# The down projection of 15 experts by seven block products, placed between the next expert's columns

## The chip, the cores and the metric

The kernel runs on one core of a Trainium2 chip. The metric is the device time of one execution in microseconds; lower is better.

## What is computed

One layer of a denoising backbone (a mixer of a long convolution and retention, then a mixture of experts, then a norm). The change is in the experts. Each of 16 experts takes the 256 latent tokens of 2048 and the 16 context tokens of 128 that have the highest affinity to it:

```python
vals, idx = lax.top_k(aff.T, cap)
xs = xt[idx]
hid = jax.nn.silu(jnp.einsum("ecd,edf->ecf", xs, p["w_e_gate"])) * jnp.einsum("ecd,edf->ecf", xs, p["w_e_up"])
ye = jnp.einsum("ecf,efd->ecd", hid, p["w_e_down"]) * vals[..., None].astype(h.dtype)
y = jnp.zeros((T, D), h.dtype).at[idx.reshape(-1)].add(ye.reshape(-1, D))
...
x = x + g2 * ec_moe(h, p)
...
y_sample = rmsnorm(xs, norm_f_g)
```

All three weights of an expert are 1024 x 1024 in float32, so the down projection is a product of 256 x 1024 by 1024 x 1024. Products are kept near float32 accuracy in three parts: an operand a is split in a rounded high part and a low part a - high, and high x high, high x low and low x high are summed.

## The kernel before

The phase of the experts (`phase_experts`) is the last of seven and takes about the last 1,250 us. Its 16 experts follow each other, unrolled in Python. On each engine `body` writes the queue of one expert by hand, and semaphores (`Steps` objects such as PW, VW, AW, VG, AH, VD, CP, one count for each named step) tie the queues together. Each engine works its queue in order.

**The columns.** The hidden side of an expert is made in eight tiles f of 128 hidden channels. For each, TensorE makes a gate column and an up column (`column`), 24 matmuls with 272 columns (256 latent and 16 context tokens) each, into PSUM banks pg and pu, from split weights (`w_high_gu`, `w_low_gu`, ring of four) and the split, transposed tokens (`xT_high`, `xT_low`). ScalarE applies silu to the gate (L3198, `act_g`); VectorE multiplies it with the up column (L3468 latent part into `full`, L3469 context part); ScalarE copies the product to its rounded high part (L3209, `hid_high`); VectorE subtracts for the low part (L3477, `hid_low`).

**The weights.** A row of weights is 128 x 1024. SP loads 24 of them for each expert in the order of STREAM (g0, u0, then g, u and the down row of the tile before). ScalarE copies each to its high part (`split`, L3151), VectorE subtracts for the low part (`split`, L3375), both two positions of the stream ahead of TensorE.

**The down projection.** `down(e, f)` adds hidden tile f times down row f to all four PSUM banks pd (2 token halves x 2 output halves), 12 matmuls of 512 columns. It stands one tile behind the columns of the same expert; the last two stand behind the context product (`down_context`, L3094, on unsplit weights). At the end of the expert VectorE multiplies the four banks by the affinity and the gate of the layer into `ye` (L3502), and the context rows likewise (L3490).

**Beside it.** In each expert VectorE also counts the places of the tokens of the expert after next (L3335, L3338, L3352), TensorE transposes the next expert's tokens, and ScalarE and VectorE split those (L3163, L3384, L3381). POOL issues the DMAs that gather tokens and that add `ye` to the sum `xacc` in memory (L3612); only when one expert's sums have landed may the next one's be issued.

**The last expert.** Once expert 14's rows are added, POOL loads `xacc` in 17 tiles (L3566). ScalarE squares each tile (L3171) and takes the root of the mean for batches of tiles (L3182), VectorE scales (L3409), POOL stores (L3570). The rows that expert 15 itself touches are done last (L3415, L3225, L3424, L3597). This work stands in the queues between the steps of expert 15's columns.

## Time and profile before

| | us |
|---|---|
| median of 3 runs | 3275.08 (3274.41 to 3278.94) |
| the profiled execution | 3273.48 |
| its span, first to last instruction | 3271.6 |
| TensorE busy in the span | 3085.6 (94%) |
| VectorE busy | 1911.9 (58%) |
| ScalarE busy | 1413.3 (43%) |

Busy times are unions of the records of an engine. A TensorE record is longer than the distance to the next one, since matmuls overlap, so prices are taken from the distance between starts. L and a number is a line of the kernel. The mean clock that TensorE was granted is 0.967 of its full rate.

### The profile page before, as it was taken

The page shows a single profiled execution, that of the slowest core. Times are in us where ns is not written, and L with a number is a line of the kernel's source. Part 1 is how long each engine was busy: PE and PEld are TensorE (multiplying, and loading weights), DVE is VectorE, ACT ScalarE, POOL GpSimd, SP SyncE. Part 2 cuts the span into 40 slices and gives each one's busy share as a digit, 9 for nine tenths or more (in the row PEclk, how much of TensorE's full clock was granted, in tenths as well). Part 3 has the DMA queues.
Part 4 walks back from the last instruction along what each step waited for, and adds up shares of the span by engine and source line. Part 5 has one row for each costly group of instructions (what it writes and reads, how often), then busy time and mean ns, then how long its engine had stood idle before and what let it go on. Part 6 is the DMA issues. An engine that isn't in the chain of part 4 may idle for free. (4 is left out here: it accounts for less than half of the span.)

```text
span 3271.6 us, 52938 instructions
## 1 busy us (share of the span) xinstructions
PE 3085.6 (94%) x20253; PEld 2673.1 (82%) x20253; DVE 1911.9 (58%) x3135; ACT 1413.3 (43%) x2101; POOL 526.9 (16%) x440
## 2 busy tenths in 40 slices
PE   7899999899979879999999984999999999999997
PEld 2378888798945779999997764999999999899996
DVE  5544443433345578776755558666666666666656
ACT  4633333422244145564644541444444444444446
POOL 1011111000023334101000003121111111112212
PEclk9999999999989889999999996999999999999998
DMA  8733332421199976767656443565655555565668
GB/s 329 264 113 114 126 106 90 153 60 60 57 313 361 362 241 219 232 218 229 216 171 202 155 149 131 197 204 193 199 195 192 193 185 183 183 208 195 198 205 311
DMA packets 334757, 630.73 MB, mean 193 GB/s; under 512 B 28408, under 2 KB 209912, under 8 KB 329865
## 3 DMA queue, kind: packets, MB, share of 16 engines
q1 hardware_dynamic: 308575, 568.47, 50.7%
q0 software_dynamic: 16992, 54.88, 5.6%
q10 hardware_dynamic: 8976, 4.46, 0.5%
q8 instruction: 143, 2.34, 0.3%
q14 instruction: 71, 0.58, 0.1%
HBM read 490.16 MB, written 137.56 MB: 192 GB/s over the span
## 5 line engine op out<-in xcount | busy, mean ns | idle before, releaser
L71 PE MATMUL experts_bank<-experts_xT_high,experts_w_high_gu 128*128 128x272 f32 x2048 | 596.2, 291 | 6.4 <-DVE experts_w_low_gu L3375 3.9
L73 PE MATMUL experts_bank<-experts_xT_high,experts_w_low_gu 128*128 128x272 f32 x2048 | 591.4, 289 | 0.0
L72 PE MATMUL experts_bank<-experts_xT_low,experts_w_high_gu 128*128 128x272 f32 x2048 | 589.6, 288 | 0.0
L71 PEld LDWEIGHTS experts_bank<-experts_xT_high,experts_w_high_gu 128*128 128x128 f32 x2048 | 386.1, 189 | 12.8 <-ACT experts_act_g L3198 5.3
L72 PEld LDWEIGHTS experts_bank<-experts_xT_low,experts_w_high_gu 128*128 128x128 f32 x2048 | 387.1, 189 | 4.6
L73 PEld LDWEIGHTS experts_bank<-experts_xT_high,experts_w_low_gu 128*128 128x128 f32 x2048 | 386.0, 188 | 0.0
L3375 DVE TENSOR_TENSOR experts_w_low_gu<-experts_w_raw_gu,experts_w_high_gu 128x1024 fp32r<-128x1024 f32 x256 | 302.6, 1219 | 25.3 <-ACT experts_w_high_gu L3151 20.5
L2146 PE MATMUL merge_bank<-merge_rows_high,merge_w_gates_high 128*128 128x272 f32 x896 | 261.4, 292 | 9.1 <-DVE merge_rows_low L2303 5.9
L3151 ACT ACTIVATE experts_w_high_gu<-experts_w_raw_gu 128x1024 fp32r<-128x1024 f32 x256 | 256.8, 1045 | 14.0 <-DMA experts_w_raw_gu<-in_w_stream 14.0
L2148 PE MATMUL merge_bank<-merge_rows_high,merge_w_gates_low 128*128 128x272 f32 x896 | 260.6, 291 | 0.0
L2147 PE MATMUL merge_bank<-merge_rows_low,merge_w_gates_high 128*128 128x272 f32 x896 | 259.2, 289 | 0.0
L73 PE MATMUL experts_bank<-experts_w_high_d,experts_hid_low 128*128 128x512 f32 x512 | 204.0, 398 | 0.0
L71 PE MATMUL experts_bank<-experts_w_high_d,experts_hid_high 128*128 128x512 f32 x512 | 203.8, 398 | 0.0
L3198 ACT ACTIVATE experts_act_g<-experts_bank 128x272 f32<-128x272 f32 x128 | 50.8, 397 | 352.4 <-PE experts_bank L73 352.3
L72 PE MATMUL experts_bank<-experts_w_low_d,experts_hid_high 128*128 128x512 f32 x512 | 202.5, 396 | 0.0
L3468 DVE TENSOR_TENSOR experts_full<-experts_bank,experts_act_g 128x256 f32<-128x256 f32 x128 | 54.4, 425 | 253.1 <-issue 150.6
L71 PE MATMUL hyin_pz<-hyin_hT_high,hyin_w_high 128*128 128x436 f32 (+1 forms) x480 | 176.2, 367 | 14.0 <-DVE hyin_hT_low L1421 14.0
L2146 PEld LDWEIGHTS merge_bank<-merge_rows_high,merge_w_gates_high 128*128 128x128 f32 x896 | 170.1, 190 | 9.8 <-issue 9.8
L3536 POOL TENSOR_TENSOR experts_spare<-experts_spare 128x1 f32<-128x1 f32 x46 | 29.0, 642 | 920.1 <-DVE experts_ye L3502 769.9
L72 PE MATMUL hyin_pz<-hyin_hT_low,hyin_w_high 128*128 128x436 f32 (+1 forms) x480 | 172.9, 360 | 0.0
L73 PE MATMUL hyin_pz<-hyin_hT_high,hyin_w_low 128*128 128x436 f32 (+1 forms) x480 | 172.9, 360 | 0.0
L2147 PEld LDWEIGHTS merge_bank<-merge_rows_low,merge_w_gates_high 128*128 128x128 f32 x896 | 170.4, 190 | 0.0
(435 smaller groups left out, 7256.4 us busy)
## 6 DMA issues: line engine op xcount, KB each, us to landing
experts_w_raw_gu<-in_w_stream SPq DMA_DIRECT2D x256, 512.0 KB, 4.6
experts_w_raw_d<-in_w_stream SPq DMA_DIRECT2D x128, 512.0 KB, 6.7
merge_rows_b<-scratch_hT SPq DMA_DIRECT2D x52, 544.0 KB, 5.4
filters_wm<-in_w_mod SPq DMA_DIRECT2D x12, 2048.0 KB, 11.2
merge_rows_t<-scratch_row_sums SPq DMA_DIRECT2D x36, 544.0 KB, 6.7
merge_y<-scratch_yhy SPq DMA_DIRECT2D x32, 544.0 KB, 5.1
merge_y<-scratch_yret SPq DMA_DIRECT2D x32, 544.0 KB, 4.7
x_early<-in_xT SPq DMA_DIRECT2D x17, 512.0 KB, 5.2
```

Of the source, the lines that this page charges most:

```text
L71: pe.matmul(out, lhs[0], rhs[0], start=start, stop=False)
L72: pe.matmul(out, lhs[0], rhs[1], start=False, stop=False)
L73: return pe.matmul(out, lhs[1], rhs[0], start=False, stop=stop)
L2146: pe.matmul(out, high, rh[:, w, q, :], start=not onto and q == 0, stop=False, skip_group_check=onto)
L2147: pe.matmul(out, high, rl[:, w, q, :], start=False, stop=False, skip_group_check=onto)
L2148: mm = pe.matmul(out, low, rh[:, w, q, :], start=False, stop=q == HK - 1, skip_group_check=onto)
L3151: act.activation(wh[kind][:, n % RINGS[kind], :], raw[kind][:, r, :], ACT.Copy).then_inc(*AW.inc(name))
L3198: act.activation(act_g[:], pg[:, 0:SLOTS], ACT.Silu).then_inc(*AG.inc(f"g{f}"))
L3375: v.tensor_tensor(wl[kind][:, w, :], raw[kind][:, n % STAGES[kind], :], wh[kind][:, w, :].bitcast(F32), ALU.subtract).then_inc(*VW.inc(name))
L3468: v.tensor_tensor(full[:, f % 2, :], pu[:, 0:CAP], act_g[:, 0:CAP], ALU.mult).then_inc(*VG.inc(f"m{f}"))
L3536: g.tensor_tensor(spare[:, column:column + 1], spare[:, 0:1], spare[:, 0:1], ALU.add)\
```

## The change

Experts 0 to 14 make the down projection as a 2 x 2 block product in seven products of quarter size instead of eight (a scheme of Strassen's kind in Winograd's form). The blocks are the two token halves and the two halves of the hidden channels of `hid` on one side, and the two halves of the hidden channels (rows f 0 to 3 and 4 to 7) and of the output channels of the weight on the other. Expert 15 keeps `down` by rows.

- A product is 4 tiles x 3 parts = 12 matmuls of 128 x 128 by 128 x 512. The seven weight operands are b11, b21, b22 (plain blocks) and t1 to t4 (sums of blocks).
- VectorE makes the four weight sums in place in the raw down rows, 128 x 4 x 512 each (`block_sum`), after the context product has read the rows. Each operand is then split in two halves of 128 x 1024 (14 splits in place of 8), in a ring of three.
- VectorE makes four sums of the hidden blocks for each of the tiles 4 to 7 (`hidden`, four instructions of 128 x 128); the high copy and the low part of these tiles are 128 x 768.
- The products of expert e stand in TensorE's queue behind columns 0, 1, 3, 5, 6, 7 and 8 of expert e + 1 (BEHIND). Products are added up in PSUM where they can be, else ScalarE copies them out (`copied`, three of 128 x 512), and VectorE adds and scales (`summed`, `gated`). The addition to memory of expert e so begins in slot 9 of expert e + 1.
- The context rows are multiplied by the gate by VectorE (four instructions of 16 x 256) and by the affinity by ScalarE.
- The stream of SP holds only gate and up rows; the eight down rows of an expert are loaded in its slots 6 to 9 (ROWS_AT). POOL gathers the tokens of the next expert before, not after, it adds the rows of the last one.
- The final tiles: new buffers, batches of 4, 4, 4 and 5, squares from slot 12 of expert 15, the tiles 8 to 16 behind its last column.

A slot i is one column (i even: gate, odd: up) and what stands behind it.

```diff
+LEAD, RING, RING_D = 2, 4, 3
+OPERANDS = ["b11", "b21", "t1", "t2", "t3", "t4", "b22"]
+PARTS = [f"{name}{i}" for name in OPERANDS for i in range(2)]
+BEHIND = {0: 0, 1: 1, 3: 2, 5: 3, 6: 4, 7: 5, 8: 6}
+SPLIT_AT = {1: [3], 2: [4, 5], 4: [6, 7], 5: [8], 6: [9, 10], 7: [11, 12], 8: [13]}
+SPLIT_NEXT = {13: 0, 14: 1, 15: 2}
+D_FIRST = (1, 6, 7, 8)
...
-        SQUARES = {1: (0, 2), 2: (2, 5), 3: (5, 8), 4: (8, 10), 5: (10, 13), 6: (13, 15)}
-        SCALED = {3: (0, 3), 4: (3, 5), 5: (5, 8), 6: (8, 10), 7: (13, NT)}
+        SQUARES = {12: (0, 4), 14: (4, 8)}
+        SCALED = {13: (0, 4), 15: (4, 8)}
+        ROWS_AT = {6: (0, 1), 7: (2, 3), 8: (4, 5), 9: (6, 7)}
+        PASSED_AT = {0: (0, 6), 1: (6, 9), 3: (9, 13), 5: (13, NLAT)}
+        DOWN_AT = {11: 0, 12: 1, 13: 2, 14: 3, 15: 4}
...
+                def block_product(e, j):
+
+                    to = pd[:, (0, 1, 2, 0, 0, 0, 2)[j], :]
+                    onto = j > 2
...
+                    for i in range(2):
+                        n = 2 * j + i
+                        w = ring_d(e, n)
+                        pe.wait_ge(VP.sem, VP.at(e, PARTS[n]))
+                        for q in (2 * i, 2 * i + 1):
+                            high, low = hh[:, q, j, :], hl[:, q, j, :]
+                            right = slice(512 * (q % 2), 512 * (q % 2) + 512)
+                            pe.matmul(to, high, dh[:, w, right], start=not onto and q == 0, stop=False, skip_group_check=onto)
+                            pe.matmul(to, high, dl[:, w, right], start=False, stop=False, skip_group_check=onto)
+                            mm = pe.matmul(to, low, dh[:, w, right], start=False, stop=q == HALF - 1, skip_group_check=onto)
+                        mm.then_inc(*DP.inc(PARTS[n]))
...
+                            else:
+                                act.wait_ge(VG.sem, VG.at(e, f"w{f}"))
+                                act.wait_ge(DP.sem, DP.at(e - 1, "b221"))
+                                act.activation(hh[:, f - HALF, 1:7, :], sums[:], ACT.Copy).then_inc(*AH.inc(f"h{f}"))
...
+                def block_sum(e, name):
+
+                    if name == "t1":
+                        for f in range(HALF):
+                            v.wait_ge(dld[f], 16 * (e + 1))
+                        v.wait_ge(PC.sem, PC.at(e, "context"))
+                        v.wait_ge(VP.sem, VP.at(e, "b111"))
+                        to, a, b = quarter("b11"), quarter("t3"), quarter("b11")
...
+                    v.tensor_tensor(to, a, b, ALU.subtract).then_inc(*TP.inc(name))
...
+                    v.tensor_tensor(sums[:, 3, :], full[:, q, 0, :], full[:, q, 1, :], ALU.subtract).then_inc(*VG.inc(f"x{f}"))
+                    done("m")
+                    v.tensor_tensor(sums[:, 1, :], full[:, q, 1, :], sums[:, 4, :], ALU.add).then_inc(*VG.inc(f"z{f}"))
+                    done("z")
+                    v.tensor_tensor(sums[:, 2, :], sums[:, 1, :], full[:, q, 0, :], ALU.subtract).then_inc(*VG.inc(f"y{f}"))
+                    done("y")
+                    v.tensor_tensor(sums[:, 5, :], sums[:, 0, :], sums[:, 2, :], ALU.subtract).then_inc(*VG.inc(f"w{f}"))
+
+                def low(e, f):
+
+                    steps = VE if final(e) else VG
+                    v.wait_ge(AH.sem, AH.at(e, f"h{f}"))
...
+                    for i in range(NS):
+                        f = i // 2
+                        if e and i == 0:
+                            block_sum(e - 1, "t1")
+                            block_sum(e - 1, "t3")
+                        for todo in splits(e, i):
+                            split(*todo)
+                        if e and i in (3, 5):
+                            block_sum(e - 1, "t2" if i == 3 else "t4")
+                        if e:
+                            evicted(e - 1, i)
...
                 def body(e, h, k, one, two):
-                    if final(e):
-                        finish(h)
-                        return
                     if one:
                         gather(e + 1, 1 - h)
-                    g.wait_ge(VD.sem, VD.at(e, "d3"))
...
+                    if e:
+                        scatter(e - 1)
+                    if final(e):
+                        finish(e % 3)
```

VectorE's queue in the middle of an expert, between hidden tiles 5 and 6 (the first row of each piece splits a weight or a token tile). Before:

```order
L3384 TENSOR_TENSOR experts_xT_low<-experts_bank,experts_xT_high 128x2x256
L3468 TENSOR_TENSOR experts_full<-experts_bank,experts_act_g 128x256
L3469 TENSOR_TENSOR experts_full_context<-experts_bank,experts_act_g 128x16
L3375 TENSOR_TENSOR experts_w_low_d<-experts_w_raw_d,experts_w_high_d 128x1024
L3477 TENSOR_TENSOR experts_hid_low<-experts_full,experts_hid_high 128x256
L3375 TENSOR_TENSOR experts_w_low_gu<-experts_w_raw_gu,experts_w_high_gu 128x1024 x2
```

Of the changed kernel, at the same place:

```order
L3494 TENSOR_TENSOR experts_w_low_gu<-experts_w_raw_gu,experts_w_high_gu 128x1024
L3566 TENSOR_TENSOR experts_hid_sums<-experts_bank,experts_act_g 128x2x128
L3567 TENSOR_TENSOR experts_full_context<-experts_bank,experts_act_g 128x16
L3572 TENSOR_TENSOR experts_hid_sums<-experts_full 128x128
L3574 TENSOR_TENSOR experts_hid_sums<-experts_full,experts_hid_sums 128x128
L3576 TENSOR_TENSOR experts_hid_sums<-experts_hid_sums,experts_full 128x128
L3578 TENSOR_TENSOR experts_hid_sums<-experts_hid_sums 128x128
L3591 TENSOR_TENSOR experts_hid_low<-experts_hid_sums,experts_hid_high 128x768
L3494 TENSOR_TENSOR experts_w_low_gu<-experts_w_raw_gu,experts_w_high_gu 128x1024
```

Between the hidden product (L3566, formerly L3468) and the low part (L3591, formerly L3477), where a weight split stood, now stand the four sums, and the low part waits for ScalarE's copy of the last of them.

VectorE's queue at the start of an expert (first the numbers of the tokens, then the output rows of the expert before). Before:

```order
L3367 TENSOR_SCALAR experts_chunk_ids<-experts_bank,experts_caps 128x1
L3490 SCALAR_TENSOR_TENSOR experts_ye<-experts_ye,experts_vals,experts_gate 16x1024
L3502 SCALAR_TENSOR_TENSOR experts_ye<-experts_bank,experts_vals,experts_gate 128x512 x4
L3375 TENSOR_TENSOR experts_w_low_gu<-experts_w_raw_gu,experts_w_high_gu 128x1024 x2
L3335 TENSOR_SCALAR experts_below<-experts_pos_slot 128x256 x2
L3338 SCALAR_TENSOR_TENSOR experts_below<-experts_pos_slot,experts_below 128x256
```

Of the changed kernel:

```order
L3487 TENSOR_SCALAR experts_chunk_ids<-experts_bank,experts_caps 128x1
L3710 TENSOR_TENSOR experts_ye<-experts_bank,experts_gate_context 16x256 x4
L3554 TENSOR_TENSOR experts_w_raw_d<-experts_w_raw_d 128x4x512 x2
L3494 TENSOR_TENSOR experts_w_low_gu<-experts_w_raw_gu,experts_w_high_gu 128x1024
L3455 TENSOR_SCALAR experts_tally<-experts_pos_slot 128x256 x2
L3458 SCALAR_TENSOR_TENSOR experts_tally<-experts_pos_slot,experts_tally 128x256 x4
L3503 TENSOR_TENSOR experts_w_low_d<-experts_w_raw_d,experts_w_high_d 128x1024
```

Two weight sums (L3554) stand ahead of the weight splits; the four outputs of 128 x 512 have gone to the slots behind their products.

ScalarE's queue in the last expert, where the first squares stand. Before (behind hidden tile 1):

```order
L3209 ACTIVATE experts_hid_high<-experts_full 128x256
L3171 ACTIVATE experts_pos_slot,experts_final_rms<-experts_final_spot 128x1024
L3171 ACTIVATE experts_pos_slot,experts_final_rms<-experts_below 128x1024
L3151 ACTIVATE experts_w_high_gu<-experts_w_raw_gu 128x1024 x2
L3198 ACTIVATE experts_act_g<-experts_bank 128x272
```

Of the changed kernel (in slot 12, behind the gate column of tile 6):

```order
L3312 ACTIVATE experts_act_g<-experts_bank 128x272
L3278 ACTIVATE experts_pos_slot,experts_final_rms<-experts_final_idle_17185 128x1024 x2
L3278 ACTIVATE experts_pos_slot,experts_final_rms<-experts_ye 128x1024 x2
L3289 ACT_TABLE_LOAD
L3289 ACTIVATE experts_final_rms<-experts_final_rms,experts_final_eps 128x4
L3242 ACTIVATE experts_w_high_gu<-experts_w_raw_gu 128x1024
L3248 ACTIVATE experts_w_high_d<-experts_w_raw_d 128x1024
```

The squares have moved from the second hidden tile to the seventh, and still stand ahead of the weight splits of the following columns.

## Rows read from the trace of the kernel before

**Rows 1.** The page: busy times of the engines, and the chain by engine.

```profile
PE 3085.6 (94%) x20253; PEld 2673.1 (82%) x20253; DVE 1911.9 (58%) x3135; ACT 1413.3 (43%) x2101; POOL 526.9 (16%) x440
...
PE 35%; DVE 1%; issue 1%; DMA 1%; ACT 0%; POOL 0%; DVEq 0%; ACTq 0%
```

**Rows 2.** Windows: length, PE, PEld, DVE, ACT, POOL busy, clock, DMA share, GB/s.

```profile
2933.60:3009.90 76.30, 76.30 (x571) 70.00 (x574) 48.03 (x82) 33.46 (x50) 13.88 (x12) 1.00 0.59 196
...
3171.60:3271.60 100.00, 79.60 (x545) 70.68 (x543) 65.78 (x84) 59.70 (x94) 31.31 (x45) 0.90 0.82 301
```

**Rows 3.** Timeline of TensorE: start, length, line, operation, form (down, then columns).

```profile
2937.61 0.40 PE L72 MATMUL experts_bank<-experts_w_low_d,experts_hid_high 128*128 128x512 f32 x1
...
2942.75 0.39 PE L73 MATMUL experts_bank<-experts_w_high_d,experts_hid_low 128*128 128x512 f32 x1
2942.98 0.29 PE L71 MATMUL experts_bank<-experts_xT_high,experts_w_high_gu 128*128 128x272 f32 x1
...
2953.38 0.29 PE L73 MATMUL experts_bank<-experts_xT_high,experts_w_low_gu 128*128 128x272 f32 x1
```

**Rows 4.** Timeline of VectorE in one expert; [idle before it <-releaser].

```profile
2941.15 2.78 DVE L3502 SCALAR_TENSOR_TENSOR experts_ye<-experts_bank,experts_vals,experts_gate 128x512 f32<-128x512 f32 x4 [0.97 <-PE experts_bank L73]
2943.85 2.35 DVE L3375 TENSOR_TENSOR experts_w_low_gu<-experts_w_raw_gu,experts_w_high_gu 128x1024 fp32r<-128x1024 f32 x2
...
2949.67 1.22 DVE L3375 TENSOR_TENSOR experts_w_low_d<-experts_w_raw_d,experts_w_high_d 128x1024 fp32r<-128x1024 f32 x1
...
2953.41 1.27 DVE L3338 SCALAR_TENSOR_TENSOR experts_below<-experts_pos_slot,experts_below 128x256 bf16<-128x256 f32 x3
...
2979.54 0.29 DVE L3381 TENSOR_TENSOR experts_xT_low<-experts_bank,experts_xT_high 128x128 fp32r<-128x128 f32 x1 [0.92 <-ACT experts_xT_high L3162]
```

**Rows 5.** Timeline of ScalarE in the same expert.

```profile
2946.48 1.05 ACT L3151 ACTIVATE experts_w_high_d<-experts_w_raw_d 128x1024 fp32r<-128x1024 f32 x1
...
2979.40 0.59 ACT L3163 ACTIVATE experts_xT_high<-experts_bank 128x512 fp32r<-128x512 f32 x1
```

**Rows 6.** Groups by line, 2080 to the end: count, busy, mean ns, idle before.

```profile
L3468 DVE TENSOR_TENSOR experts_full<-experts_bank,experts_act_g 128x256 f32<-128x256 f32 x122 | 51.9, 425 | 240.6 <-issue 141.3 <-PE experts_bank L73 98.6 <-ACT experts_act_g L3198 0.6
...
L3209 ACT ACTIVATE experts_hid_high<-experts_full 128x256 fp32r<-128x256 f32 x122 | 51.0, 418 | 240.8 <-DVE experts_full L3468 240.8
```

**Rows 7.** One line's instructions (another stage): min/median/max ns.

```profile
L1438 DVE TENSOR_TENSOR hyin_u<-hyin_c x4: 3982/3986/3989, 649.7 to 887.3; 128x2048 f32<-128x2048 f32 x4
```

**Rows 8.** Timeline of POOL, ScalarE and VectorE in the last expert.

```profile
3172.67 1.10 POOL L3536 TENSOR_TENSOR experts_spare<-experts_spare 128x1 f32<-128x1 f32 x1 [50.98 <-DVE experts_ye L3502]
...
3188.33 0.19 POOL L3536 TENSOR_TENSOR experts_spare<-experts_spare 128x1 f32<-128x1 f32 x1 [7.59 <-DMA scratch_xacc<-experts_ye,experts_sids]
...
3193.38 1.06 ACT L3171 ACTIVATE experts_pos_slot<-experts_final_spot 128x1024 bf16<-128x1024 f32 x1 [8.59 <-DMA experts_final_spot<-scratch_xacc]
...
3194.63 1.06 ACT L3171 ACTIVATE experts_pos_slot<-experts_below 128x1024 bf16<-128x1024 f32 x1
...
3211.32 1.28 DVE L3409 SCALAR_TENSOR_TENSOR experts_final_spot<-experts_final_spot,experts_final_rms,experts_gf 128x1024 f32<-128x1024 f32 x1
...
3220.36 1.28 ACT L3182 ACT_TABLE_LOAD   x1
...
3267.87 0.96 POOL L3597 DMA_INDIRECT out_y_sample<-experts_ye,experts_sids x1 [0.63 <-DVE experts_ye L3424]
```

**Rows 9.** Windows of 1 us in the last expert; the third number from the end is the clock.

```profile
3195.00:3196.00 1.00, 0.43 (x2) 0.00 (x0) 0.00 (x0) 1.00 (x3) 0.69 (x2) 1.00 1.02 385
...
3198.00:3199.00 1.00, 0.87 (x4) 0.90 (x5) 1.00 (x1) 0.90 (x1) 0.00 (x0) 0.50 1.00 410
...
3201.00:3202.00 1.00, 1.00 (x8) 1.00 (x8) 0.05 (x1) 0.97 (x2) 0.00 (x0) 0.84 1.05 418
...
3235.00:3236.00 1.00, 0.38 (x2) 0.00 (x0) 0.77 (x1) 1.00 (x2) 0.00 (x0) 1.00 0.96 393
3236.00:3237.00 1.00, 0.40 (x3) 0.43 (x4) 1.00 (x2) 1.00 (x3) 0.25 (x1) 1.00 1.03 418
```

631 lines of the change are left out of this document (390 added, 241 removed).

## The prediction

> **What bounds the kernel now.** I read the page's busy shares and chain first. TensorE is busy for 94% of the span and the chain consists of its matmuls [rows 1]. The windows then say where VectorE stands: in one expert of 76.3 us TensorE is busy for all of it, VectorE for 48.0, ScalarE for 33.5 [rows 2]. The TensorE timeline gives the prices: starts of 272-column matmuls lie 0.125 us apart ((2953.38 - 2942.98) / 83), those of 512-column ones 0.2336 ((2942.75 - 2937.61) / 22) [rows 3]. In the timelines of the other engines the reader is to see the price of each kind of instruction by its width [rows 4, 5], and in the grouped view that VectorE and ScalarE wait for TensorE: 240.6 us before the hidden product, 240.8 before its rounded copy, over 122 of them each [rows 6]. They have about 28 us of slack per expert. The question is whether the change fits into it.
>
> **TensorE's part.** The down projection of one expert is 8 x 12 = 96 matmuls of 512 columns now and 7 x 12 = 84 then; nothing else goes from TensorE. 12 x 0.2336 = 2.8 us, so 73.5 us are left of 76.3 in experts 1 to 14. If TensorE stayed the bound, 14 x 2.8 = 39 us would be gained there.
>
> **VectorE's part, expert by expert.** An instruction occupies the engine some 0.08 us less than its record lasts (two 1024-wide subtractions take 2.35, one 1.22, so one is 1.13 [rows 4]). By that:
> - low halves of the down weights: 14 operand halves in place of 8 rows, 6 x 1.13 = +6.8;
> - four weight sums of 4 x 512 = 2048 elements. No row has this form. Twice the 1024-wide one is 2.2 us (lower end); the upper end is 3.99, the 2048-wide product of another stage [rows 7], but that one reads both inputs with a step of 32 elements, and the sums read runs of 512. I take 2.2: +8.8;
> - hidden side: for four of the eight hidden tiles, four sums of 128 elements (a 128-wide record is 0.29, so 0.20 each): 16 x 0.20 = +3.2; the low half is 768 wide instead of 256 for these four (0.34 to 0.87) and 128 wide for the others (0.34 to 0.20): +1.6;
> - outputs: four products with gate and weight become three additions and four such products on 512 elements (0.60 and 0.68, the 2.78 of four [rows 4]): +1.8; for the context rows four instructions of 256 elements (0.34 each, as the hidden product's 425 ns record [rows 6]) stand for one of 1024 (1.13 at least): +0.2.
>
> Together +22.4. One expert before occupies VectorE for 46.5 us (the 48.0 busy less the record tails before idle time), so 68.9 then. That alone would still fit under 73.5.
>
> **The handovers.** But VectorE's and ScalarE's queues are in program order and wait for each other several times in each expert. Now this lies in VectorE's slack. When VectorE itself is late, every such wait is lost time, because what stands behind it is queued. I lay VectorE's list of one expert end to end:
> - hidden tiles 4 to 7: the third and fourth sum each wait for the one before (0.13 x 2); then VectorE waits for ScalarE's 768-wide copy (between 0.42 for 256 [rows 6] and 1.05 for 1024 [rows 5]: 0.85, and 0.04 at each side, 0.09 end of the sum: 1.02) and only then makes the low half. 4 x 1.28 = 5.1;
> - hidden tiles 0 to 3: 128-wide copy, 0.37 each, 1.5;
> - behind each low half stands a weight split, whose rounded copy (1.04) ScalarE starts only after its hidden copy, since it too waited for VectorE: 0.75 four times, 0.08 four times, and 0.50 more in the two slots where it first copies a product out of PSUM (0.59 record [rows 5]): 4.3;
> - slot 7: ScalarE waits for a product, then copies it and rounds the operand half that VectorE waits for: 1.3;
> - the second weight sum waits for the first, three additions are followed by their own products: 4 x 0.13 = 0.5.
>
> 12.7 in all, 68.9 + 12.7 = 81.6, and in slots 9 and 11, where VectorE has least to do, it waits 0.6 for TensorE: **82.2 us per expert, with VectorE and not TensorE as the bound**. TensorE then idles 8.7 us per expert, in two spaces of some 2.2 us (before second halves of products, whose operand is still being split) and four shorter ones.
>
> **The sum.** Expert 0 has no product beneath its columns: 96 x 0.2336 = 22.4 less, and 1.4 more for the wait before the index matmuls: -21.0. Experts 1 to 13: 13 x (82.2 - 76.3) = +76.7. Expert 14 doesn't count the places for a later one, 16 x 0.395 = 6.3 us of VectorE (three take 1.27 [rows 4]): 75.9, -0.4. Expert 15: its columns began at 3171.64 and the end came 100.0 later [rows 2]. Now expert 14's rows are added to memory before its columns, POOL needing 3188.33 - 3172.67 = 15.7 us for it [rows 8]. In the changed kernel the last block is ready only in slot 9, about 52 us into expert 15; the sum in memory is complete at 68. The first tile can be squared 5 us later (3188.33 to 3193.38 [rows 8]), at 73, and ScalarE, which has these squares in its queue ahead of the weight splits, stands until then and TensorE behind it. Four squares 1.25 apart (3193.38 to 3194.63) and their root with its table load of 1.28 [rows 8] make 6.6: 79. From there VectorE has 17 scaled tiles (1.20 of the 1.28 each [rows 8], 20.4), two weight splits (2.3), three row splits (3.4), two hidden tiles (2.4), context (1.4), three residuals (3.6), four outputs (2.7) and three last rows (4.5): 40.7, some 4 of waits, and 3.7 from the last store's issue to the end [rows 8]: 127.5. +27. The total is -21.0 + 76.7 - 0.4 + 27 = +82. The profiled execution took 3273.48 (span 3271.6), 1.6 below the median of 3275.08; I add to the median: **3357 us**.
>
> **What the skill says.** What a weight sum costs is open between the rows, 2.2 (from 1.22 at 1024 elements [rows 4]) and 3.99 [rows 7]. The Trainium skill, "VectorE: DVE Perf Modes", section "The TRN2 errata", gives a two-input fp32 instruction (N + 151) / 0.96 ns: 2.29 us at 2048 is the estimate by that page, and the sum would stay at +82; by rows 7 it would be +177. Its section "Rules for kernel authors" advises few instructions on this engine, which speaks against a change that adds some 35 per expert.
>
> **Rivals.**
>
> A, *TensorE stays the bound, faster.* VectorE's 68.9 are below 73.5, and if its queue ran ahead in light slots the handovers would vanish. Then 73.5 per expert: -21 - 39 + 27 and less = 3242, or about 3220 if the end is short too. Against it: 12.7 us of handovers are fixed by the order, and nothing in the list lets VectorE run ahead of a hidden tile. 5%.
> B, *partly hidden.* 76.5 to 80 per expert, if records overlap more than I take (VectorE 5 to 8% cheaper): expert 14 again 6.3 below the others: 3275 - 21 + 13 x (0.2 to 3.7) - (6.1 to 2.6) + 27 = 3278 to 3327. 12%, of which 3% within 0.2%.
> C, *the clock, slower still.* TensorE was granted the half rate (0.50, 1.2 GHz) for 3.9 us behind an idle time of 2.7 us (TensorE busy until 3195.43, and again from 3198.13), and kept 2.4 GHz after one of 1.2 us [rows 9]. The two spaces of 2.2 us lie between. If each sets the clock back, its 2 us of matmul time lost are partly covered: +1.0 to 1.7 per expert, 13 x 1.3 = +17, 3374; 3390 at most. The Trainium skill, "TensorE: Matmul & The Clock Gate", section "What's actually happening", says that activity gives the array its full rate and idleness takes it back; the rows at 3198 and 3201 agree. 18%.
> D, *the sums cost 3.99.* 4 x 1.7 = 6.8 more per expert, 14 x 6.8 = 95: 3452. 4%.
> E, *the seven products or the smaller staging hold up a transfer.* Weight loads are issued a whole ring ahead, and no wait of rows 4 to 6 is for one; the change moves eight row loads into four slots of 5 us, 1.5 MB each, some 310 GB/s in SP's queue, above the mean of 196 now but near the 301 that the last 100 us moved [rows 2]. If late, 3400. The gather, which POOL now issues first, gains time that no row shows as missing. 3%.
>
> **Numbers.** My forecast, 3330 to 3370 about 3357, has 58%; A 5, B 12, C 18, D 4, E 3. The range 3300 to 3395 leaves out A, D, E and the low end of B. A measurement of this kernel tells some 0.2% (6.5 us) from no change. Faster 0.06, within 0.2% 0.03, slower 0.91.
>
> **What would show it.** In the changed profile: a middle expert of 82 us with VectorE at 70 and TensorE at 73 to 75 busy; VectorE's idle time put down to ScalarE's hidden and weight copies and hardly to TensorE; the sums at 2.29; TensorE waiting for VectorE's low halves; the last expert above 120 us, with a wait of ScalarE for the first tile. I am wrong if an expert takes 73 to 76 with VectorE's waits still at TensorE, or if the sums' row shows another price.

## The result, and the profile after the change

Over the same runs the kernel before took 3274.76 us and the changed one 3372.93 (medians), a ratio of 1.0297 with a 95% interval of 1.0279 to 1.0315: 98 us slower. 3357 was forecast, with a range of 3300 to 3395. The profiled execution has a span of 3368.9 us, 97.3 more than the 3271.6 before.

The page of the changed kernel answers [rows 1]: first the busy times, then the chain by engine.

```profile
PE 3071.1 (91%) x20073; PEld 2652.7 (79%) x20073; DVE 2272.1 (67%) x3618; ACT 1512.3 (45%) x2184; POOL 509.4 (15%) x440
...
DVE 18%; PE 16%; ACT 3%; issue 2%; DMA 1%; POOL 0%; DVEq 0%; ACTq 0%; POOLq 0%
```

The chain that belonged to TensorE now lies on VectorE as much as on TensorE (18% and 16% of the span). VectorE did 360 us more (2272.1 against 1911.9) and TensorE 14.5 less.

Windows answer [rows 2] (columns: stretch, length, busy time of PE, PEld, DVE, ACT, POOL, granted clock, DMA share, GB/s). The first two are experts in the middle, from the start of one context product to the start of the next, the third is expert 14, the last goes from the first column of expert 15 to the end.

```profile
2246.26:2330.09 83.83, 77.52 (x557) 70.18 (x555) 72.03 (x115) 40.40 (x57) 13.55 (x12) 0.96 0.55 177
2579.29:2661.99 82.70, 74.82 (x557) 68.03 (x554) 72.01 (x115) 40.38 (x57) 13.75 (x12) 1.00 0.56 181
3160.45:3235.65 75.20, 74.04 (x552) 67.74 (x550) 64.50 (x96) 39.11 (x56) 14.27 (x12) 1.00 0.61 196
3240.04:3368.90 128.86, 96.32 (x632) 85.07 (x628) 94.90 (x114) 70.73 (x106) 30.01 (x45) 0.90 0.69 245
```

An expert takes 82.7 us in place of 76.3; TensorE is busy for 74.8 of it and stands for 7.9. One expert in three takes 83.8, and these are the ones with a mean clock of 0.96.

Who waits for whom in the expert of 82.70: the list of waits, VectorE first, then TensorE (us in total, times, longest).

```profile
DVE experts_hid_low L3591 <- ACT experts_hid_high L3330: 3.7, 4, 0.9
DVE experts_w_low_d L3503 <- ACT experts_w_high_d L3257: 2.8, 3, 1.1
DVE experts_w_low_gu L3494 <- ACT experts_w_high_gu L3242: 1.8, 2, 1.1
DVE experts_hid_low L3591 <- ACT experts_hid_high L3326: 1.2, 4, 0.3
DVE experts_hid_sums L3566 <- PE experts_bank L73: 0.4, 1, 0.4
```

```profile
PE experts_bank L3146 <- DVE experts_w_low_d L3503: 3.5, 3, 2.5
PE experts_bank L3146 <- ACT experts_ye L3264: 2.1, 1, 2.1
PE experts_bank L71 <- DVE experts_full_context L3567: 1.3, 1, 1.3
PE experts_bank L3091 <- DVE experts_xT_low L3599: 1.0, 1, 1.0
```

VectorE waits 9.5 us for ScalarE and only 0.4 for TensorE. Before, it and ScalarE waited for TensorE almost alone [rows 6]. ScalarE in its turn stands for VectorE (it is busy for half the time): neither is full, each stands for the other. That is what a bound by handovers looks like: no engine at 100%.

The timeline of VectorE in the same expert answers [rows 4] (start, length, line, operation, tiles, form, count, [idle before it <-releaser]):

```profile
2582.47 0.29 DVE L3578 TENSOR_TENSOR experts_hid_sums<-experts_hid_sums 128x128 f32<-128x128 f32 x1
2583.68 0.96 DVE L3591 TENSOR_TENSOR experts_hid_low<-experts_hid_sums,experts_hid_high 128x768 fp32r<-128x768 f32 x1 [0.92 <-ACT experts_hid_high L3330]
...
2584.82 1.76 DVE L3710 TENSOR_TENSOR experts_ye<-experts_bank,experts_gate_context 16x256 f32<-16x256 f32 x4
2586.61 4.77 DVE L3554 TENSOR_TENSOR experts_w_raw_d<-experts_w_raw_d 128x2048 f32<-128x2048 f32 x2
2591.29 1.22 DVE L3494 TENSOR_TENSOR experts_w_low_gu<-experts_w_raw_gu,experts_w_high_gu 128x1024 fp32r<-128x1024 f32 x1
...
2598.91 0.29 DVE L3591 TENSOR_TENSOR experts_hid_low<-experts_full,experts_hid_high 128x128 fp32r<-128x128 f32 x1 [0.29 <-ACT experts_hid_high L3326]
2600.34 1.23 DVE L3494 TENSOR_TENSOR experts_w_low_gu<-experts_w_raw_gu,experts_w_high_gu 128x1024 fp32r<-128x1024 f32 x1 [1.14 <-ACT experts_w_high_gu L3242]
...
2604.89 2.29 DVE L3554 TENSOR_TENSOR experts_w_raw_d<-experts_w_raw_d 128x2048 f32<-128x2048 f32 x1
2607.09 0.69 DVE L3511 TENSOR_TENSOR experts_ye<-experts_bank,experts_ye 128x512 f32<-128x512 f32 x1
```

The two handovers of the prediction stand in it: 0.92 idle before the 768-wide low half, 0.29 before the 128-wide one, and 1.14 behind that, before the next weight split. The two lines with x4 and x2 are taken up below.

Set against the prediction's sum, from first columns (2026.03, 2104.12 and 3171.64 before; 2026.83, 2084.46, 3164.03 and 3240.04 after; before, one expert is (3171.64 - 2104.12) / 14 = 76.25):

| Part | forecast, us | measured, us |
|---|---|---|
| expert 0, with the wait ahead of it | -21.0 | 58.4 - 78.1 = -19.7 |
| experts 1 to 13 | +76.7 | 1079.6 - 991.3 = +88.3 |
| expert 14 | -0.4 | 76.0 - 76.25 = -0.2 |
| expert 15 to the end | +27 | 128.9 - 100.0 = +28.9 |
| sum | +82 | +97.3 |

So 15 us are missing, and 11.6 of them lie in the thirteen middle experts. There two things have to be told apart: 0.5 us more in every expert (82.7 for 82.2), and 1.1 in every third.

### The profile page after: what moved, and what is told of

Same layout as the page of the kernel before. It is cut to its first block and busy times, and to the rows that moved or that the text cites. A ratio compares the mean times of both kernels' runs of the same rounds, so it can differ in the third digit from the quotient of the medians.

```text
span 3368.9 us, 53322 instructions
## 1 busy us (share of the span) xinstructions
PE 3071.1 (91%) x20073; PEld 2652.7 (79%) x20073; DVE 2272.1 (67%) x3618; ACT 1512.3 (45%) x2184; POOL 509.4 (15%) x440
## 5 line engine op out<-in xcount | busy, mean ns | idle before, releaser
L71 PE MATMUL experts_bank<-experts_xT_high,experts_w_high_gu 128*128 128x272 f32 x2048 | 603.6, 295 | 11.7 <-DVE experts_full_context L3567 9.4
L3494 DVE TENSOR_TENSOR experts_w_low_gu<-experts_w_raw_gu,experts_w_high_gu 128x1024 fp32r<-128x1024 f32 x256 | 312.1, 1219 | 53.0 <-ACT experts_w_high_gu L3242 48.1
L3503 DVE TENSOR_TENSOR experts_w_low_d<-experts_w_raw_d,experts_w_high_d 128x1024 fp32r<-128x1024 f32 x210 | 251.2, 1220 | 46.8 <-ACT experts_w_high_d L3257 46.8
L3242 ACT ACTIVATE experts_w_high_gu<-experts_w_raw_gu 128x1024 fp32r<-128x1024 f32 x256 | 268.6, 1049 | 12.6 <-DMA experts_w_raw_gu<-in_w_stream 12.6
L3146 PE MATMUL experts_bank<-experts_w_high_d,experts_hid_high 128*128 128x512 f32 x420 | 174.7, 416 | 73.9 <-DVE experts_w_low_d L3503 46.3
L3257 ACT ACTIVATE experts_w_high_d<-experts_w_raw_d 128x1024 fp32r<-128x1024 f32 x210 | 214.0, 1048 | 0.0
L3326 ACT ACTIVATE experts_hid_high<-experts_full 128x128 fp32r<-128x128 f32 x60 | 18.6, 310 | 338.0 <-DVE experts_full L3566 338.0
L2148 PEld LDWEIGHTS merge_bank<-merge_rows_high,merge_w_gates_low 128*128 128x128 f32 x896 | 169.1, 189 | 0.0
L3148 PE MATMUL experts_bank<-experts_w_high_d,experts_hid_low 128*128 128x512 f32 x420 | 168.8, 402 | 0.0
```

The source lines that it names most:

```text
L71: pe.matmul(out, lhs[0], rhs[0], start=start, stop=False)
L2148: mm = pe.matmul(out, low, rh[:, w, q, :], start=False, stop=q == HK - 1, skip_group_check=onto)
L3146: pe.matmul(to, high, dh[:, w, right], start=not onto and q == 0, stop=False, skip_group_check=onto)
L3148: mm = pe.matmul(to, low, dh[:, w, right], start=False, stop=q == HALF - 1, skip_group_check=onto)
L3242: act.activation(gh[:, n % RING, :], raw_gu[:, n % RING, :], ACT.Copy).then_inc(*AW.inc(STREAM[n]))
L3257: act.activation(dh[:, w, :].rearrange("p (a b) -> p a b", b=512), part_of(e, n), ACT.Copy).then_inc(*AD.inc(PARTS[n]))
```

## The experiments

The theory that the runs test (Q in the expectations): VectorE's queue, with its own work and the handovers with ScalarE laid end to end, sets the length of an expert. The rivals: TensorE, the clock, VectorE's busy time without regard to order. All kernels are edits of the changed one. "Per expert" is the mean distance of the starts of the context product (line L3177) over experts 1 to 13; the changed kernel has (3160.45 - 2080.89) / 13 = 83.04 by it.

**1. Is it VectorE, and how far?** The weight sums all but gone:

```diff
-v.tensor_tensor(to, a, b, ALU.subtract)
+v.tensor_tensor(to[:, 0:1, 0:8], a[:, 0:1, 0:8], b[:, 0:1, 0:8], ALU.subtract)
```

> The four weight sums of each expert are made over 8 elements in place of 2048 (the rest of the sums is left out, so the products use other weights); every wait, product and transfer stays. Theory Q (VectorE's queue sets an expert's 83.1 us): the row of the weight sums falls from 2.29 us to some 0.07, VectorE is relieved of 4 x 2.1 = 8.4 us, and the expert falls by 6 to 7 us to 76 to 77, where waits for TensorE take over; 3373 - 13 x 6.6 - 2 = about 3285. Rival C (the half clock behind TensorE's gaps stretches the expert): the gaps behind the split operands stay, so no more than 2 us per expert comes off, 3345 or more. Rival P (TensorE or the transfers bound it): no change, 3373.

Measured: 3277.66 us, 1.0005 of the kernel before (0.9996 to 1.0015), 76.02 per expert. The group of the sums by form (count, busy, mean ns, idle before), in the changed kernel and in this one:

```profile
L3554 DVE TENSOR_TENSOR experts_w_raw_d<-experts_w_raw_d 128x2048 f32<-128x2048 f32 x60 | 138.0, 2299 | 2.5
```

```profile
L3554 DVE TENSOR_TENSOR experts_w_raw_d<-experts_w_raw_d 128x8 f32<-128x8 f32 x60 | 10.4, 174 | 2.5
```

4 x 2.12 = 8.5 us less work gave 7.0 us. The sums, the piece of the change that looks like a detail, are worth more than all that TensorE saves by it (2.8). And with them gone the kernel stands where it stood before: the rest of the added work still eats the whole gain.

**2. Is it TensorE?** A third of the block products' matmuls left out:

```diff
-pe.matmul(to, high, dl[:, w, right], ..., stop=False, ...)
-mm = pe.matmul(to, low, dh[:, w, right], start=False, stop=q == HALF - 1, ...)
+mm = pe.matmul(to, high, dl[:, w, right], start=False, stop=q == HALF - 1, ...)
```

> The third matmul (low half of the hidden sum times rounded weight) is left out of the seven products: 84 - 28 = 56 matmuls of 512 columns per expert, 28 x 0.2336 = 6.5 us less for TensorE; VectorE and ScalarE do all they did. Theory Q (VectorE's queue): only the place where ScalarE and VectorE wait for a product (slot 7) is sooner ready, so 0 to 1.2 us per expert come off: 3356 to 3373, and TensorE's idle time grows by 5 to 6.5 us per expert. Rival P (TensorE bounds): 6.5 us per expert come off, 3373 - 14 x 6.5 = 3282. Rival C: with shorter work between the gaps the clock falls at least as often, 3373 or more.

Measured: 3367.61 us (1.028, 1.0263 to 1.0297), 82.60 per expert. TensorE's waits in one expert of it, to be held against the four lines above:

```profile
PE experts_bank L3146 <- DVE experts_w_low_d L3502: 5.3, 3, 3.9
PE experts_bank L3146 <- ACT experts_ye L3263: 2.8, 1, 2.8
PE experts_bank L3091 <- DVE experts_xT_low L3598: 1.7, 1, 1.7
PE experts_bank L71 <- DVE experts_full_context L3566: 1.2, 1, 1.2
```

6.5 us of matmuls less per expert, 0.4 us less time; TensorE waits 11.0 in place of 7.9 (the rest goes to the half clock: the mean clock of that expert is 0.96). Rival P would have needed 3282 and is out. It is also the other face of the change: that it saves matmuls is worth next to nothing here.

**3. Are the handovers real costs, or slack that only shows as waits?** Nothing is taken out; in odd slots VectorE makes the slot's last weight split between the hidden sums and the hidden low half, while ScalarE makes the rounded copy that the low half needs:

```diff
-for todo in splits(e, i):
+todos = splits(e, i)
+held = [todos.pop()] if i % 2 and todos else []
+for todo in todos:
     split(*todo)
...
     hidden(e, f)
...
+    for todo in held:
+        split(*todo)
     low(e, f)
```

> On VectorE alone, in every odd slot, the slot's last weight split is moved from ahead of the hidden product to between the hidden sums and the hidden low half; nothing is added or left out. Handover theory (12.7 us of each expert are waits between VectorE and ScalarE, made only by the order): the wait of 0.92 before the 768-wide low half and that of 0.29 before the 128-wide one vanish under 1.13 us of split, and the wait behind it falls from 0.66 to nothing and from 1.14 to 0.5: 83.1 falls by 5 to 5.5 us to 77.6 to 78.1 per expert, 3373 - 13 x 5.2 - 7 = about 3298; the last expert's tail gains up to 5 us of it. Rival B (VectorE's plain busy time of 72 us and some fixed chain set the expert, the waits are slack): the waits only move, within 1 us per expert, 3360 to 3373. If the later low halves of the weights come too late for TensorE, slower than 3373.

Measured: 3295.64 us (1.0061, 1.0045 to 1.0078), 77.61 per expert. Timeline of VectorE at such a place:

```profile
2526.84 0.29 DVE L3578 TENSOR_TENSOR experts_hid_sums<-experts_hid_sums 128x128 f32<-128x128 f32 x1
2527.05 1.22 DVE L3494 TENSOR_TENSOR experts_w_low_gu<-experts_w_raw_gu,experts_w_high_gu 128x1024 fp32r<-128x1024 f32 x1
2528.18 0.95 DVE L3591 TENSOR_TENSOR experts_hid_low<-experts_hid_sums,experts_hid_high 128x768 fp32r<-128x768 f32 x1
2529.05 1.22 DVE L3494 TENSOR_TENSOR experts_w_low_gu<-experts_w_raw_gu,experts_w_high_gu 128x1024 fp32r<-128x1024 f32 x1
```

No idle time is left in it, and the same instructions in another order are 5.4 us per expert faster (5.1 against the experts of 82.7; the other 0.3 is the clock of run 7, which stayed at 1.00 here). This is 77 us of the 98 that the change cost. The busy time hardly moved (71.1 in place of 72.0), so a rival that counts busy time alone can't explain it.

**4 and 5. How far does order go?** The counts of places for the expert after next (6.3 us of VectorE, needed only at the end of an expert) are moved to other slots, once with the edit of 3 and once alone:

```diff
-PASSED_AT = {0: (0, 6), 1: (6, 9), 3: (9, 13), 5: (13, NLAT)}
+PASSED_AT = {0: (0, 2), 3: (2, 4), 5: (4, 6), 9: (6, 10), 10: (10, 12), 11: (12, NLAT)}
```

> As e3_split_before_low, and the 16 counts of places (6.3 us of VectorE) stand in slots 0, 3, 5 (two each), 9 (four), 10 (two) and 11 (four) in place of 0, 1, 3 and 5. Theory: VectorE's queue is late only in slots 0 to 8, where it also makes the sums; in slots 9 and 11 it waits for TensorE by 1.3 to 1.6 us as soon as e3's waits are gone. Then the move is worth 2 to 2.5 us per expert beyond e3: 75.0 to 75.8 per expert, below the 76.3 of the kernel before, about 3268 (expert 0 loses 3). If the sum of VectorE's work over an expert is what counts and not where it stands, e4 equals e3 within 5 us.

> From the changed kernel: only the 16 counts of places are moved, to the slots that e4 has them in; the weight splits stay ahead of the hidden products. With e3 and e4 this makes a square of two changes. Theory: as long as the handover waits keep VectorE late in every slot, it waits in slots 9 and 11 for TensorE by 0.6 us only, so the move is worth 0.6 to 0.8 us per expert (82.7 to 82.0) and loses 3 to 4 in expert 0: 3364 to 3370. In e4 against e3 the same move was worth 2.6 per expert. If the place of the counts had a worth of its own, 2.6 per expert here too, 3338. The experts of 83.8 with two clock falls may stay.

Measured: with the edit of 3, 3262.54 us (0.9956, 0.9939 to 0.9972), 75.05 per expert; alone, 3364.20 (1.0261, 1.0243 to 1.0280), 81.99. The same move is worth 2.6 us per expert behind the other one, and 1.05 on the changed kernel, where no expert took 83.8 any more; against the 82.7 of the others it is 0.7. What moving work to a light slot brings depends on whether that slot is light: in slots 9 and 11 VectorE waited 1.6 and 1.2 us for a column of TensorE's in the kernel of run 3, and 0.4 and 0.1 in the changed one. So with nothing but its order altered the changed kernel comes out below both.

**6. The remaining waits filled.** The counts where VectorE stood for ScalarE's operand halves:

```diff
-PASSED_AT = {0: (0, 2), 3: (2, 4), 5: (4, 6), 9: (6, 10), 10: (10, 12), 11: (12, NLAT)}
+PASSED_AT = {1: (0, 2), 2: (2, 3), 3: (3, 7), 6: (7, 10), 7: (10, 14), 9: (14, 16)}
```

> As e4_and_counts_later (62 rows of VectorE's order as in e3), but the 16 counts of places stand in slots 1 (two), 2 (one), 3 (four), 6 (three), 7 (four) and 9 (two): in the slots where VectorE stands waiting for ScalarE's operand halves or for a block (1.9 us before slot 7's halves, 1.2 before slot 9's block in e4's order), and none in slot 11, where TensorE had to wait 0.8 us for a low half. Theory Q: the handover waits are filled, TensorE never waits but 0.4 us before the index products, and the expert falls from 74.93 to 73.8 us, which is TensorE's own 73.4; 3262.5 - 13 x 1.1 - 2.8 in expert 0 = about 3245, below both kernels. If TensorE's 73.4 cannot be reached (its blocks then lie closer to the halves being split), 74.9 stays and 3262.

Measured: 3251.64 us (0.9919, 0.9905 to 0.9932), 74.23 per expert, where 73.8 had been expected. The windows of two experts of it:

```profile
2304.68:2379.02 74.34, 73.55 (x557) 67.96 (x555) 70.93 (x115) 40.51 (x57) 16.48 (x12) 1.00 0.61 201
2527.30:2600.99 73.69, 73.59 (x557) 67.97 (x554) 70.86 (x115) 40.45 (x57) 16.01 (x12) 1.00 0.61 202
```

In the second of them TensorE is the bound again, at the 73.5 us that the prediction gives its part; VectorE is busy for 70.9 of 73.7 and no longer in the way. This is the best kernel of the study, 0.8% below the one before. The 6 us between 3245 and 3252 lie in waits for a weight load. By the starts single experts took between 73.6 and 75.2, and in nine of the thirteen ScalarE waits for a gate or up row to land, 65 to 71 us into the expert. The longest expert, of 75.18, has the longest wait, 1.45; the shortest, of 73.64 and 73.69, have none:

```profile
2671.86 1.06 ACT L3242 ACTIVATE experts_w_high_gu<-experts_w_raw_gu 128x1024 fp32r<-128x1024 f32 x1 [1.45 <-DMA experts_w_raw_gu<-in_w_stream]
```

These waits add up to 6.5 us over the thirteen experts. Once the handovers are gone, the transfers are the next thing that a faster expert meets.

**7. The clock.** In the changed kernel, windows of 1 us around one of TensorE's two long waits, first around the wait in slot 1 in one expert, then around the one in slot 6 in the next expert; the clock is third from the end:

```profile
2178.00:2179.00 1.00, 0.00 (x0) 0.00 (x0) 1.00 (x4) 0.00 (x0) 0.83 (x1) 1.00 0.64 213
...
2182.00:2183.00 1.00, 1.00 (x6) 1.00 (x6) 0.85 (x3) 0.17 (x1) 0.00 (x0) 0.50 0.54 82
...
2185.00:2186.00 1.00, 1.00 (x10) 1.00 (x9) 1.00 (x2) 1.00 (x2) 0.00 (x0) 1.00 0.00 0
```

```profile
2288.00:2289.00 1.00, 0.00 (x0) 0.00 (x0) 0.71 (x4) 0.50 (x2) 0.00 (x0) 1.00 0.00 0
...
2292.00:2293.00 1.00, 1.00 (x3) 0.72 (x3) 1.00 (x2) 0.42 (x2) 0.00 (x0) 0.50 0.00 0
```

Behind a wait of 2.5 us the clock fell to 0.50 (1.2 GHz) in two of three experts, behind the second, of 2.1, in one of three. Where only the first fell, the expert took 82.70 like one with no fall (TensorE was busy for 76.2 us in place of 74.8, and nobody waited for it). Where the second fell, ScalarE got product 4 later, and the longest wait of VectorE for its rounded copy went from 1.1 to 2.2:

```profile
DVE experts_w_low_d L3503 <- ACT experts_w_high_d L3257: 4.0, 3, 2.2
```

That is the 1.1 us of the 83.8. The test gives TensorE something to do in both waits, 16 matmuls per expert that nobody reads:

```diff
+def fill(e, n):
+    h = (e + 1) % 2
+    for q in range(8):
+        pe.matmul(pd[:, 3, :].rearrange(...), xh[:, h, 2, 0:P], xh[:, h, 0:2, 0:CAP], start=q == 0, stop=q == 7, ...)
...
+if j == 4:
+    fill(e, 2 * j - 1)
...
+if (j, i) == (1, 1):
+    fill(e, n - 1)
```

> From the changed kernel: TensorE gets 8 matmuls of 512 columns into an unused bank (1.87 us) ahead of each of its two long waits per expert (before the second half of product 1 in slot 1, before product 4 in slot 6); nobody reads them. In the changed kernel the granted clock fell to 0.50 behind one of these waits in some experts and behind both in every third, and only those with both took 83.8 us against 82.7. Theory: the idle times shrink from 2.5 and 2.1 to 0.7 and 0.2 us, the granted clock stays at 1.00 and all experts take 82.7: 4 x 1.1 less, 3369, although TensorE does 3.7 us more per expert. Rival C as predicted (the clock costs 1.0 to 1.7 in every expert): 13 x 1.3 less, 3356. Rival P (TensorE bounds): 14 x 3.7 more, 3425.

Measured: 3369.07 us (1.0287, 1.0272 to 1.0303), 82.72 per expert, every one between 82.67 and 82.78:

```profile
2409.56:2492.26 82.70, 78.59 (x573) 70.91 (x570) 72.01 (x115) 40.36 (x57) 13.56 (x12) 1.00 0.56 180
```

TensorE does 3.8 us more per expert and the kernel is 4 us faster by its medians. That is within their scatter, but the experts show it: from first column to first column experts 1 to 13 took 1075.4 us in place of 1079.6, with no fall of the clock in them. Experts 14 and 15, where VectorE has less to do, grew by 1.7 and 1.6 with the matmuls added. The clock's share of the 98 us is 4 x 1.1 = 4.4.

**8. The 0.5 us in every expert.** Of the two lines pointed to in the timeline, the four context products take 2586.61 - 2584.82 = 1.79 us, 0.45 from start to start, though one lasts only 0.42; the prediction gave them 0.34, the distance at which a 256-wide product is followed elsewhere. They are the only instructions of VectorE in an expert that start on the partitions 0, 32, 64 and 96 in turn.

```diff
-rows = slice(32 * c, 32 * c + CCAP)
+rows = slice(0, CCAP)
```

> From the changed kernel: the four products of the context rows read the partitions 0 to 15 of the bank and of the gate four times in place of 0, 32, 64 and 96 (so three quarters of the context rows' values are left out and the first quarter stands in their place); width, count and waits stay. In the changed kernel the four take 1.79 us (2584.82 to 2586.61), 0.445 from start to start, longer than their record of 0.418; the prediction had 0.34 each, as a 256-wide product has elsewhere. Theory H (a product that starts on other partitions than the one before it waits until that has ended, and pays some 0.1 us): 4 x 0.34 = 1.36 and the one behind them starts earlier, so 0.4 to 0.5 us per expert come off, 82.7 to 82.25, about 3366. Rival (the form itself, 16 partitions of a bank by a wide tile, is that slow): no change.

Measured: 3360.43 us (1.0256, 1.0239 to 1.0274), 82.10 per expert (82.03 from the second on). The same place in VectorE's timeline:

```profile
2579.88 1.40 DVE L3710 TENSOR_TENSOR experts_ye<-experts_bank,experts_gate_context 16x256 f32<-16x256 f32 x4
2581.20 4.69 DVE L3554 TENSOR_TENSOR experts_w_raw_d<-experts_w_raw_d 128x2048 f32<-128x2048 f32 x2
2585.82 1.22 DVE L3494 TENSOR_TENSOR experts_w_low_gu<-experts_w_raw_gu,experts_w_high_gu 128x1024 fp32r<-128x1024 f32 x1
```

1.32 in place of 1.79, 0.33 each: theory H holds, and the rival (the form is slow) is out. The kernel gained more than the 3366 expected. An expert fell by 0.67 and not by 0.4 to 0.5: by the starts 0.46 lies in the four products, 0.08 in the weight sum right behind them and 0.11 in a wait before the hidden product of slot 1. The costly fall of the clock, behind the wait in slot 6, came in the first of these experts only (82.91); the others are alike, six of them with a fall behind the wait in slot 1, which is 2.0 us now. The Trainium skill, "VectorE: DVE Perf Modes", section "Two Vector instructions with no wait between them", has the rule: an instruction whose inputs or output start in another group of 32 partitions than those of the last instruction that read or wrote the same memory starts only when all before it have finished. The trace agrees, 0.45 against 0.33 us from start to start; the prediction had not used it.

**9. The last expert.** Expert 14's down projection made by rows as expert 15's is, within and just behind expert 14 (the core of the edit; the order of the output tiles' squares goes with it):

```diff
+BYROW = LAST - 1
...
-if e and i in BEHIND:
+if e and e < LAST and i in BEHIND:
     block_product(e - 1, BEHIND[i])
-if final(e) and i in DOWN_AT:
-    down(DOWN_AT[i])
+if byrow(e) and i in DOWN_AT[e == LAST]:
+    down(e, DOWN_AT[e == LAST][i])
```

> From the changed kernel: expert 14's down projection is made by rows too, inside expert 14 and just behind it, as expert 15's is (13 experts by seven products left, from 0 to 12, and expert 13's products in expert 14 as before); its sum in memory starts before expert 15's columns, the tiles' squares stand in slots 8 and 13. The prediction's step: +27 in the last expert because the sum of expert 14 is complete only 68 us into it. Theory: then expert 15 takes about 108 from its first column (128.9 now), but expert 14 takes 97.9 in place of 75.2 to 76, since it holds both expert 13's products (19.6) and its own rows (22.4), so the time stays within 0.2% of 3373 (3371): three quarters of the last expert's +29 is TensorE work of expert 14 moved behind expert 15's first column, the rest is lateness of the sum. Rival: if lateness of the sum alone made the +29, expert 15 falls by 21 and expert 14 grows by less than that, and some 3350 would come out.

Measured: 3374.83 us (1.0305, 1.0289 to 1.0321). Expert 14 and expert 15 from their first columns:

```profile
3165.22:3262.93 97.71, 96.06 (x650) 85.76 (x646) 71.15 (x94) 47.68 (x65) 14.99 (x12) 1.00 0.49 159
3262.93:3370.30 107.37, 76.45 (x545) 70.00 (x543) 67.50 (x87) 58.52 (x90) 31.96 (x45) 0.86 0.79 286
```

97.7 and 107.4, for 97.9 and 108 expected. Expert 15 gets 21.5 us shorter and expert 14 21.7 longer. So the +28.9 of the last expert and the -19.7 of expert 0 are for the most part one and the same thing: the down projection of each expert moved one expert later, and the 19.6 us of expert 14's products now lie in expert 15. Of the last expert some 9 us are a loss. The run takes the late sum and the 19.6 us of products away together, so it doesn't say what either is worth alone. But with its sum complete 14 us after the first column (3277.15 - 3262.93), expert 15 still takes 7.4 us more than in the kernel before; where these lie is not shown.

The place of the loss was then sought in ScalarE's stand for the first output tile, on the kernel of 6:

```diff
-SQUARES = {12: (0, 4), 14: (4, 8)}
+SQUARES = {13: (0, 4), 14: (4, 8)}
```

> As e5_counts_spread, and in the last expert the first eight squares of output tiles stand behind slots 13 and 14 of ScalarE's list in place of 12 and 14. The prediction's step: ScalarE stands in slot 12 until the first tile is there (4.85 us in the changed kernel, with VectorE idle for 14.7 and TensorE behind it). Theory: one slot more of splits is done before ScalarE stands, so TensorE's last columns come earlier by 2 us, but the tiles are scaled by as much later and VectorE's list from the first tile to the end stays as long: 1 to 2 us less, 3250. If ScalarE's stand were the whole of the last expert's excess, 5 or more would come off.

Measured: 3251.16 us (0.9918, 0.9904 to 0.9931), no difference from 3251.64 that can be told. The windows from the first column of expert 15 to the end, in the kernel of 6 and in this one, say more:

```profile
3122.56:3249.81 127.25, 94.28 (x632) 83.58 (x628) 94.39 (x113) 69.98 (x106) 30.54 (x45) 0.90 0.70 247
3123.91:3247.73 123.82, 94.01 (x632) 83.66 (x628) 94.53 (x113) 70.01 (x106) 32.36 (x45) 0.90 0.70 254
```

The last expert is 3.4 us shorter, where 1 to 2 had been expected. The time of the whole doesn't show it, since in this execution the experts began 3.2 us later (first column at 2030.01 in place of 2026.82), behind stages that the edit doesn't touch; one execution of each can't tell more. ScalarE's wait of 5.15 us for the first tile is gone, and the context product of expert 15 stands 84.7 us behind its first column in place of 88.2. So the stand is worth 3.4 us here, less than the 5 or more that would have made it the whole loss; from the context product to the end both take 39 us.

## Why the prediction was right, point by point

- **TensorE's part, and that it would not stay the bound**: right. With 84 matmuls an expert's TensorE work is 73.5 us, measured as such in run 6 (busy for 73.6), and TensorE idles 7.9 us per expert (8.7 forecast) in two spaces of 2.5 and 2.1 (2.2 each) and shorter ones. Run 2 shows it directly.
- **VectorE's work**: right in size. Busy for 72.0, where "VectorE at 70" was to show it. The weight sums, open between 2.2 and 3.99, are 2.299 by their group and 2.2 as occupied (2604.89 to 2607.09); rival D is out. The Trainium skill's figure for them, cited in the prediction from "VectorE: DVE Perf Modes", was 2.29.
- **The handovers**: right. 12.7 us were forecast. 9.5 show as waits for ScalarE; with the waits of VectorE for itself and the 0.08 that a record's tail covers they come to 12.4 in the expert of 82.70, by the distances between starts. 1.02 was forecast between the end of the last hidden sum's occupied time and the low half; the rows give 2583.68 - 2582.67 = 1.01. Run 3 shows that these waits were a cost and not slack: 5.4 us per expert for a change of order alone.
- **82.2 per expert**: the step that was mis-sized, at 82.7. It is the term "+0.2" for the context rows, four instructions "of 0.34 each": they are 0.45 (run 8), +0.43, and the second of the two sums that follow each other started 0.28 and not 0.13 behind the first's occupied time (4.68 for the pair, not 4.53), +0.15. Smaller terms give back 0.1. 13 x 0.5 = 6.5 of the missing 15 us. With the partitions alike the expert took 82.03.
- **Rival C, the clock**: its mechanism came true, its price didn't. Falls came in two of three experts, but the half rate costs nothing where VectorE is late anyway; only the fall that delays the one product ScalarE waits for costs 1.1. 13 x 1.3 = 17 was asked, 4.4 it was. The 3.9 us of half rate that it read in the kernel before are 3.4: the clock is 0.96 from 3197.00 to 3198.00, 0.50 from there on and 0.84 from 3201.00 to 3202.00, so a fall takes 1.7 us of matmul time and not 2. The prediction held it for another case (18%) and it belonged into the main one as a small term.
- **Expert 0**: -19.7 for -21.0. The wait before the index matmuls was 0.98 us, where 1.4 had been given, but the first column starts 0.8 us later (2026.83 for 2026.03) and the half clock at the start, which the prediction had left out, lasts for 4.3 us of matmuls where it lasted 3.4 before. Some 0.5 us are not traced.
- **The last expert**: +28.9 for +27. The sum in memory was complete 65.6 us after the first column (68 forecast), the first tile was squared at 69.4 (73), the root was done at 77.1 (79), so ScalarE's stand and the wait of the sum in memory are as told; from there to the end it took 51.8 and not 48.4. The two errors have opposite signs and partly cancel, which is luck. Of the 3.4 us more, none is VectorE's work: it was busy for 40.6 us, 40.7 forecast. Its waits were 6.0 in place of 4; the longest is 3.4 us for a row split that stands behind four squares and a table load on ScalarE. The last store was issued 1.3 us behind VectorE's last result, since POOL issues two others just before it, which the forecast had left out, and took 3.9 to the end in place of 3.7. The first square and that row split on ScalarE, then the wait on VectorE:

```profile
3309.43 1.06 ACT L3278 ACTIVATE experts_pos_slot<-experts_final_idle 128x1024 bf16<-128x1024 f32 x1 [4.85 <-DMA experts_final_idle<-scratch_xacc]
...
3330.30 1.04 ACT L3248 ACTIVATE experts_w_high_d<-experts_w_raw_d 128x1024 fp32r<-128x1024 f32 x1
```

```profile
3331.37 1.23 DVE L3499 TENSOR_TENSOR experts_w_low_d<-experts_w_raw_d,experts_w_high_d 128x1024 fp32r<-128x1024 f32 x1 [3.43 <-ACT experts_w_high_d L3248]
```

  What the prediction did not see is that +27 and -21 are mostly one displacement (run 9); its sum has both, so its result doesn't suffer.
- **Rivals A, B and E**: out. VectorE's waits are for ScalarE; no wait of TensorE, VectorE or ScalarE in the middle experts is for a transfer, and the DMA share is 0.56. A came near only in the kernel of run 6, whose order was changed (74.23 per expert, single ones at 73.6), and there waits for a weight load, a late transfer as in E, cost up to 1.45 us in an expert.

The errors, 6.5 for the two terms in the expert, 4.4 for the clock, 0.7 for 76.25 in place of 76.3, 1.3, 0.2 and 1.9 for the experts 0, 14 and 15, add up to the missing 15.

## What to carry to other kernels

Before work is moved to an engine that looks idle, lay its queue end to end with every wait for the other engines: a handover that costs nothing in slack costs its full length once the engine is late, and busy shares of 87% (DVE) and 49% (ACT) can be a bound. When the added work is nearly as long as the bound it is to relieve, put an independent instruction between what one engine hands over and what it takes back, and do it together with the change: here order alone turned 3% slower into 0.8% faster. A change that shifts work by one stage shows as a gain at the start and a loss at the end; count both before calling either an effect.

## What the runs showed that had not been expected

- The four context products, which begin on other partitions each time, follow each other at 0.45 us; on the same partitions at 0.33. With what follows from it this is 0.67 us per expert, and with the clock 12 us of the kernel (3372.9 to 3360.4).
- The granted clock fell behind a wait of 2.5 us in two experts of three and behind one of 2.1 in one of three, in a steady pattern of three experts. Why three is open. In run 8 it fell behind waits of 2.0 us too. Filling the waits with matmuls that nobody reads kept it at 1.00 and cost nothing in experts 1 to 13, but 1.7 us in expert 14, where TensorE is busy for 74.0 of 75.2 us.
- The last of an engine's excess work is hard to win back by removing work: with 8.5 us of sums gone the expert stood at 76.0, 2.5 above TensorE's own 73.5, while the order of run 6 reached 73.7 with all the work in it.
